# The second layer's modulation moves from the first routing stage into the heads of the first attention

## The reference, cut to what matters

```python
for i in range(2):                                   # layers of the first block
    mod_l = cond_lat @ w_mod[i] + b_mod[i]           # 1 x 6144, split in six
    mod_c = cond_ctx @ w_mod[i] + b_mod[i]
    a_lat = rmsnorm(x, norm_mix_g[i]) * (1 + sc1) + sh1
    y_lat = mla(a_lat, a_ctx) if i == 0 else short_conv(a_lat)   # 8 heads; 256 queries, 512 keys
    x = x + g1 * y_lat
    f_lat = rmsnorm(x, norm_ffn_g[i]) * (1 + sc2) + sh2
    x = x + g2 * hier_moe(f_lat)                     # softmax routing, 32 experts, top 2
...
```

## Time and profile before

| | |
|---|---|
| device time, median of 3 executions | 2698.28 us (2694.34 to 2699.42) |
| the profiled execution | 2698.76 us, span 2697.0 us |
| TensorE products (PE) | 2328.4 us busy, 86% of the span |
| TensorE weight loads (PEld) | 1548.8 us, 57% |
| VectorE (DVE) | 1045.7 us, 39% |
| ScalarE (ACT) | 717.4 us, 27% |
| GpSimd (POOL) | 170.6 us, 6% |
| mean granted TensorE clock | 0.914 of full |
| HBM read | 613.76 MB, 228 GB/s over the span |

### The profile page before, as it was taken

One profiled execution on the slowest core, in us unless ns is written; L12 is line 12 of the kernel. 1 busy time (PEld: TensorE's weight loads), 2 busy tenths in 40 slices (PEclk: granted clock), 3 DMA queues, 4 the chain that ended last, 5 costly groups with the idle time before them and its releaser, 6 DMA issues. The chain is left out here.

```text
span 2697.0 us, 31599 instructions
## 1 busy us (share of the span) xinstructions
PE 2328.4 (86%) x13732; PEld 1548.8 (57%) x13732; DVE 1045.7 (39%) x1713; ACT 717.4 (27%) x1028; POOL 170.6 (6%) x118
## 2 busy tenths in 40 slices
PE   4887799999999784999999979955499989858988
PEld 1633534444444682444444449933389889747988
DVE  3323221111111542111111145733659836654983
ACT  3122211111111431111111135611235424223551
POOL 0000000000000000000000000021005400000540
PEclk7999799999999896999999989965599999988999
DMA  7713599999996433999999925500045443401542
GB/s 260 234 63 125 191 411 421 421 419 398 400 401 246 172 120 152 407 399 398 401 400 398 396 96 187 170 20 0 0 136 183 166 174 132 150 1 63 188 172 79
DMA packets 197633, 616.95 MB, mean 229 GB/s; under 512 B 19952, under 2 KB 82672, under 8 KB 148080
## 3 DMA queue, kind: packets, MB, share of 16 engines
q1 hardware_dynamic: 190416, 610.96, 59.4%
q10 hardware_dynamic: 7072, 3.88, 0.5%
HBM read 613.76 MB, written 1.05 MB: 228 GB/s over the span
## 5 line engine op out<-in xcount | busy, mean ns | idle before, releaser
L517 PE MATMUL bank<-normed_rounded,ring_rounded 128*128 128x256 f32 x3784 | 478.6, 288 | 23.2 <-ACT normed_rounded L581 16.4
L517 PEld LDWEIGHTS bank<-normed_rounded,ring_rounded 128*128 128x128 f32 x3784 | 467.1, 193 | 33.4 <-issue 20.2
L1136 PE MATMUL bank<-ring,arena 128*64 128x512 f32 x2048 | 450.4, 592 | 1.6 <-DVE arena L1500 1.6
L294 DVE TENSOR_TENSOR ring_rounded<-ring,ring_rounded 128x4096 fp32r<-128x4096 f32 (+2 forms) x74 | 326.5, 4416 | 191.5 <-ACT ring_rounded L288 191.5
L517 PE MATMUL bank<-arena_rounded,ring_rounded 128*128 128x256 f32 (+1 forms) x2576 | 359.4, 297 | 33.6 <-ACT arena_rounded L609 12.3
L517 PEld LDWEIGHTS bank<-arena_rounded,ring_rounded 128*128 128x128 f32 x2576 | 334.2, 196 | 50.9 <-ACT arena_rounded L609 14.6
L1136 PEld LDWEIGHTS bank<-ring,arena 128*64 128x64 f32 x2048 | 147.4, 137 | 292.8 <-issue 290.8
L288 ACT ACTIVATE ring_rounded<-ring 128x4096 fp32r<-128x4096 f32 (+2 forms) x74 | 259.7, 3514 | 76.0 <-DMA ring<-in_ffn_w_down 52.9
L1505 DVE TENSOR_TENSOR arena<-arena,bank 64x512 f32<-64x512 f32 x64 | 43.4, 679 | 578.5 <-ACT arena L1337 578.5
L1145 PE MATMUL bank<-ring,arena 128*64 128x512 f32 x1024 | 233.8, 598 | 0.0
L505 PEld LDWEIGHTS bank<-mats,arena 128*128 128x128 f32 (+1 forms) x900 | 117.8, 185 | 101.1 <-issue 79.5
(11 more groups left out here) (222 smaller groups left out, 1870.0 us busy)
## 6 DMA issues: line engine op xcount, KB each, us to landing
ring<-in_moe_w_gate SPq DMA_DIRECT2D x128, 1024.0 KB, 8.6
ring<-in_moe_w_up SPq DMA_DIRECT2D x128, 1024.0 KB, 10.8
ring<-in_moe_w_down SPq DMA_DIRECT2D x128, 1024.0 KB, 7.9
ring<-in_w_mod SPq DMA_DIRECT2D x24, 2048.0 KB, 13.0
ring<-in_ffn_w_up SPq DMA_DIRECT2D x44, 1024.0 KB, 7.4
ring<-in_ssm_w_in SPq DMA_DIRECT2D x12, 2048.0 KB, 8.0
ring<-in_ffn_w_down SPq DMA_DIRECT2D x10, 2048.0 KB, 7.9
ring<-in_conv_w_in SPq DMA_DIRECT2D x6, 2048.0 KB, 9.2
```

The lines of the kernel that those rows point to most:

```text
L294: e.tensor_tensor(ring.rounded[slot][:, 0:n].bitcast(F32R), ring.slots[slot][:, 0:n], ring.rounded[(self.number + 1) % RING][:, 0:n], ALU. ...
L517: end = e.matmul(out, lhs.bitcast(F32R), rhs.bitcast(F32R), start=start and n == 0 and k == 0, stop=stop and n == 2 and k == n_k - 1)
L1136: ends[i] = e.matmul(bank[rows, :], self.xt[x][:, j, n * cap:(n + 1) * cap], weights[:, j, :], start=n == 0 and j == 0, stop=n == 1 and j ...
```

## The change

The twelve steps of layer 1 become a third `Modulation`, `self.ahead` in `Mla`, and the five last steps of layer 0 and these twelve are dealt to the heads in order, two to a head (three in head 7). The first of a head's steps stands where the one step stood, between `scores(h + 1)` and `values(h)`; the second stands inside `values(h)`, between the transposes of the probabilities and the product with V. Head 2 holds the last step of layer 0 with its closing turn, and then step 0 of layer 1. `Moe` of layer 0 has no steps any more. `w_ukv`, whose slot of the ring is read by every head, is *kept*: `fetch` skips that slot until `kept` is cleared behind the `w_o` chunks. The rows of layer 1's steps are held in `late` (two buffers) in place of two in the arena.

```diff
 class Ring:
     def restart(self):
+        self.kept = set()
...
 class Chunk:
     def fetch(self, e, w):
         ring = self.ring
+        while {(ring.number + n) % RING for n in range(2 if self.split else 1)} & ring.kept:
+            ring.number += 1
         self.number = ring.number
...
+    def keep(self):
+        self.ring.kept.add(self.number % RING)
...
 class Modulation:
-    def __init__(self, k, layer, first, steps, row):
+    def __init__(self, k, layer, first, steps, row, *busy):
+        self.busy = busy
...
         if at - 2 >= self.first:
             w.wait_ge(*k.pe.at("mod turn", self.layer, at - 2))
+        elif self.busy:
+            w.wait_ge(*k.pe.at(*self.busy[at - self.first]))
...
 class Mla:
+        self.ahead = Modulation(k, 1, 0, 12, lambda at: late[at % 2], ("mod turn", 0, 10), ("mod turn", 0, 11))
+        between = [(self.rest, at) for at in range(7, 12)] + [(self.ahead, at) for at in range(12)]
+        self.between = [between[2 * h:2 * h + 2 if h < MLA_HEADS - 1 else None] for h in range(MLA_HEADS)]
...
     def sync(self, e, w):
         self.w_ukv.fetch(e, w)
-        for at in range(7, 12):
-            self.rest.fetch(e, w, at)
+        self.w_ukv.keep()
+        for modulation, at in sum(self.between, []):
+            modulation.fetch(e, w, at)
         for chunk in self.w_o:
             chunk.fetch(e, w)
+        k.ring.kept.clear()
...
     def tensor(self, e, w):
+        def steps(h, which):
+            for modulation, at in self.between[h][which]:
+                modulation.step_tensor(e, w, at)
+                if modulation is self.rest and at == 11:
+                    modulation.close_tensor(e, w)
+
         def values(h):
...
                 end.then_inc(*pe.up("pt", h, q))
+            steps(h, slice(1, None))
             bank, emptied = banks.next(dve, "o", h)
...
                 scores(h + 1)
-            if h < 5:
-                self.rest.step_tensor(e, w, 7 + h, turn=True)
+            steps(h, slice(0, 1))
             values(h)
-        self.rest.close_tensor(e, w)
+        self.ahead.close_tensor(e, w)
...
     def scalar(self, e, w):
         for h in range(MLA_HEADS):
-            if h < 5:
-                self.rest.step_scalar(e, w, 7 + h)
+            steps(h, slice(0, 1))
             if h == MLA_HEADS - 1:
                 self.w_o[0].round_scalar(e, w)
             values(h)
+            steps(h, slice(1, None))
             if h + 1 < MLA_HEADS:
                 softmax(h + 1)
-        w.wait_ge(*pe.at("mod turn", 0, 11))
+        w.wait_ge(*pe.at("mod turn", 1, 11))
         self.w_o[1].round_scalar(e, w)
...
 class Moe:
-        self.ahead = None
-        if layer == 0:
-            mod_rows = [ar.take(512), ar.take(512)]
-            self.ahead = Modulation(k, 1, 0, 12, lambda at: mod_rows[at % 2])
...
     def sync(self, e, w):
-        if self.ahead:
-            for at in range(12):
-                self.ahead.fetch(e, w, at)
...
     def tensor(self, e, w):
-        fill(0, 2)
...
-        fill(2, 5)
...
-        fill(7, 5)
-        if self.ahead:
-            self.ahead.close_tensor(e, w)
```

More of the change, by code:

```diff
@@ L715, in sync @@
     def sync(self, e, w):
+        k = self.k
         for at in range(3):
@@ L907, in values, with steps @@
                              ACT.Copy).then_inc(*act.up("pt", h, q))
+        def steps(h, which):
+            for modulation, at in self.between[h][which]:
+                modulation.step_scalar(e, w, at)
         w.wait_ge(*dve.at("turned", (1, 5)))
@@ L1005, in values, with sums @@
             dve.mark("o", h)
+        def sums(modulation, at):
+            modulation.step_vector(e, w, at)
+            if at == 11:
+                modulation.close_vector(e, w)
         self.rest.step_vector(e, w, 5)
@@ L1012, in vector @@
                 key_part(h + 1)
-            if h < 5:
-                self.rest.step_vector(e, w, 6 + h)
+            for modulation, at in self.between[h - 1] if h else [(self.rest, 6)]:
+                sums(modulation, at)
             if h == MLA_HEADS - 1:
@@ L1019, in vector @@
                 softmax(h + 1)
-        self.rest.step_vector(e, w, 11)
-        self.rest.close_vector(e, w)
+        for modulation, at in self.between[-1]:
+            sums(modulation, at)
         self.w_o[1].rest_vector(e, w)
@@ L1167, in tensor @@
         k.meet(w, self.before)
-        def fill(first, n):
-            if self.ahead:
-                for at in range(first, first + n):
-                    self.ahead.step_tensor(e, w, at)
-        fill(0, 2)
         n_log = GROUPS + EXPERTS
@@ L1302, in scalar @@
                     ).then_inc(*self.router.up("router"))
-        def fill(first, n):
-            if self.ahead:
-                for at in range(first, first + n):
-                    self.ahead.step_scalar(e, w, at)
         w.wait_ge(*dve.at("mod", layer, 4 if layer == 0 else 0))
@@ L1324, in scalar @@
             e.activation(x, x, ACT.Exp).then_inc(*act.up(key, "exp", name))
-        fill(2, 10)
         def rows(x):
@@ L1378, in vector @@
             e.tensor_scalar(self.slots[:, n * cap:(n + 1) * cap], count[:, 0:cap], 1.0, None, ALU.add).then_inc(*dve.up())
-        def fill(first, n):
-            if self.ahead:
-                for at in range(first, first + n):
-                    self.ahead.step_vector(e, w, at)
-        fill(0, 1)
         n_log = GROUPS + EXPERTS
@@ L1453, in vector @@
         tt(by_token[:, 1], by_token[:, 1], self.tmp, ALU.add)
-        fill(1, 5)
         bank = banks.of(key, "ranks")
@@ L1485, in vector @@
         places(1)
-        fill(6, 6)
-        if self.ahead:
-            self.ahead.close_vector(e, w)
         def turned_back(x):
```

## The result

| | before | changed |
|---|---|---|
| median, first measurement | 2698.28 us | 2712.29 us (2705.70 to 2715.73, 5 runs) |
| ratio | | 1.0048, 95% interval 1.0030 to 1.0066 |
| second measurement, another chip | 2700.03 us (25 runs) | 2706.49 us (2703.11 to 2715.34, 12 runs) |
| ratio | | 1.0028, 95% interval 1.0012 to 1.0044 |
| profiled execution | 2698.76 us, span 2697.0 | 2708.74 us, span 2706.9 |

The change makes the kernel slower, by 14.0 us in one measurement and 6.5 in the other; 6.8 was forecast. The first value lies 0.3 us outside the forecast's range, the second well inside it. (The ratios are estimated over the runs; they are not exactly the quotients of the two medians.) I read the profiled pair (10.0 us apart) from the stages that were changed to those that were not.

A forecast was written before the change was run, and what follows sets the result against it. It took the attention as bound by a chain through all engines, layer 0's routing first by the router's transfers. Attention +20.7, routing -12.9, convolution start -6.2, layer 1's logits +5.2: +6.8, thus 2705.6 profiled, median 2705.1 us; range 2696 to 2712.

The forecast's parts named there:

- A step ahead costs 2.4: In an attention head, a step placed ahead of the transposes costs 2.4 us, with nothing hiding it.
- A second step costs 1.7: In heads 0, 1, 3 and 4, a step behind the transposes: 2.44 us less 0.74 of TensorE's wait, 1.7 each.
- Head 2: Closing turn waiting for a ScalarE copy, some 0.8 us, then a step without a turn, 1.2: 2.0 in all.
- a head that gets both: Heads 5 and 6, without steps before, get one ahead of and one behind the transposes: 4.1 us each, 8.2 together.
- I had let the clock only gain: Rival: fuller attention heads lose their half-clock stretches, -5.1 us, giving 2700.0; chance 0.22.
- The heads together: All added steps in the attention's heads cost 17.0 us, bounds 15 and 19.
- The end of the attention: w_o's second chunk lands 9.3 us after issue, delaying rounding and TensorE's return by 3.7 us; bounds 2.3 and 7.3.
- The routing of layer 0: Without steps, 35.5 us from logits to first expert; router lands 19.4 after issue, 2.4 later than before: gain 12.9.
- The Trainium skill's rule: Router of layer 0: larger neighbouring rows would delay its landing to 329.7, making the sum 5.2 us higher than forecast.
- The ring's shift: Convolution's first chunk comes earlier, gaining 6.2 us; two more halves ahead of layer 1's router cost 5.2.
- The sum: Whole kernel: 20.7 - 12.9 - 6.2 + 5.2 = +6.8 us on the profiled 2698.76.

The follow-up runs named there:

- b1: Changed kernel with both layers' router weights fetched at the start of the attention, into a free end of the arena: 2657.32 us (0.9843).
- b2: Kernel before the change with both layers' router weights fetched at the start of the attention: 2659.55 us (0.9861).
- c3: Changed kernel with w_o's second chunk in ring slots 0 and 1, so twelve expert halves are issued ahead of the router: 2714.02 us (1.0060).
- a2: Changed kernel with the ring moved one slot on behind the attention, so the convolution's first chunk is in slot 5 again: 2711.96 us (1.0046).
- a3: Kernel before the change with only the ring moved one slot back, so the convolution's first chunk goes to slot 4: 2697.79 us (0.9998).
- a1: Changed kernel measured again, unaltered, on another chip against the kernel before: 2706.49 us (1.0028).
- b4: Changed kernel with both steps of each head ahead of the transposes, none between them and the product with V: 2716.93 us (1.0063).
- a4: Changed kernel with the first steps of heads 0 to 6 moved between the next head's key product and its scores: 2684.22 us (0.9951).
- b3: Changed kernel with first steps between key product and scores, and router weights fetched at the start of the attention: 2639.24 us (0.9783).
- c4: Changed kernel with first steps between key product and scores, router weights fetched early, and w_o's second chunk in slots 0 and 1: 2634.55 us (0.9762).
- c1: Kernel before the change with its five head steps moved between the next head's key product and its scores: 2686.12 us (0.9948).
- c2: Kernel before the change with its head steps between key product and scores, and router weights fetched early: 2644.05 us (0.9802).

## Why the forecast held, point by point

- *A step ahead costs 2.4.* Held: 14.2 - 11.7 = 2.5, and nothing under the key wait.
- *A second step costs 1.7.* Too much: 15.5 - 14.2 = 1.35 at full clock. The 0.74 of ScalarE's wait went as expected, and 0.35 more. The rows place it: from its start to the product with V the second step with its turn takes 188.12 - 185.77 = 2.35 and not 2.44, the wait it fills is 0.81 from start to start, the product with V itself is 0.10 shorter without a wait ahead of it, and the wait ahead of the scores is 2.65 in place of 2.75. Four heads give 5.4 in place of 6.8. Head 2 gave 2.0 as forecast (17.81, less 1.6 for the clock and 14.2), and a head that gets both 15.53 - 11.71 = 3.8 in place of 4.1.
- *The heads together.* From head 1's scores to head 7's it is 14.2 us more (100.26 against 86.09); the forecast's terms for this stretch give 12.9. Steps at full clock account for 5.4 + 2.0 + 3.8 = 11.2, and the half-clock stretches, four of 1.6 in place of two of 1.7, for 3.0. That the stretches grow in number stands in none of my rivals: I had let the clock only gain. So two errors stood against each other here, steps 1.7 too dear and stretches left out; that the total came near is luck.
- *The end of the attention.* The second chunk landed 7.7 us after its issue, not 9.3, and was waited for by 4.78 us. From head 7's scores to TensorE's return it takes 35.9 us in place of 30.0, of which 3.8 are head 6's steps: 2.1 for the end where 3.7 was forecast and 2.3 was the lower bound. With 7.7 in place of 9.3 the forecast's own sum gives the 2.1. The mean at the end of the stage, L550 before and L560 now, is 21.6 us later, 0.9 of which the execution brought along from its start: 20.7, as forecast. It came out of parts that were each a little off: 18.0 for the heads with head 6, not 17.0; 2.1 for the end, not 3.7; and 0.6 from TensorE's return to the mean (23.9 against 23.3), where nothing was forecast. That the whole fits to the tenth is luck.
- *The routing of layer 0.* From the router's issue to the first expert 54.4 us in place of 67.8: 13.4 gained, 12.9 forecast. Landing 19.5 (19.4 forecast), 34.9 from there (35.5). That steps lay under the router's wait is shown by b1 and b2, as 6.4 us.
- *The Trainium skill's rule* (DMA: Bandwidth & Descriptors, Queues, rings and completion order). The page states that an engine changes between queues by whole packets. The prediction concluded from it that the router would land 24.6 us after its issue, as in layer 1, because of the larger rows beside it. It landed after 19.5. The halves are the same ones in both layers and in c3, and the landing of the larger transfer goes from 19.5 to 29.5 us with the number of halves in line, so here the end of the backlog decided. The rule is not refuted: the smaller transfer took no longer behind twelve halves than behind ten, and among the w_mod chunks with their smaller rows both came through sooner. No run here varied the rows' size with the backlog held.
- *The ring's shift.* -6.0 at the convolution's start (the mean comes 896.86 - 883.11 = 13.75 us behind the last row of the experts, L1184 now, in place of 19.7) and +5.0 in layer 1, both as forecast, and both shown by a2 and a3 one at a time.
- *The sum.* 20.7 - 13.4 - 6.0 + 5.0 = +6.3. The profiled pair shows 8.0 at layer 1's first expert less the 0.9 of its start, so 7.1; the convolution took 1.2 more in this execution, from its mean to the router's issue, and from the logits to layer 1's first expert it was 0.4 less. Behind that the pair differs by 2.0 in untouched stages. The first measurement's 14.0 is not explained by the sum: no trace is kept of its other executions, so that the rest lies in the clock and in untouched stages is likely from the spread, and not shown.

## What to carry to other kernels

Work that is dealt out to idle time costs nothing only where the idle time ends last. In these heads TensorE was idle for a quarter of the time; a step behind the scores cost its full length, and the same step a few instructions earlier, ahead of the wait for the key copy, cost nothing. Where work is moved out of a stage, ask what wait had covered it: the twelve steps were worth 19.8 us in the routing and gave 13.4, because a small transfer behind a large backlog was late either way, and that transfer, not the steps, was the 40 us to be had. And a moved slot of a shared ring reaches stages that the change does not name.

## What I had not expected of the hardware

- The half-clock stretches follow the bare waits of about 2.7 us, not the amount of work. Head 1's scores wait 1.6 us, those of heads 2 to 7 wait 2.65 to 2.75. Of these six waits three were followed by a stretch at half clock in the kernel before and five in the changed kernel; the same attentions in other profiled executions have three (a3) and four or five (a1, a2). With the same work and six waits of 2.75 us (b4) it was three. Behind a filled wait there was none, in a4, b3 and c4 as in c1 and c2. What is left there stands behind a wait of 2.65 to 2.75 that had stayed: one stretch each in a4, b3 and c4 with one such wait, one in c1 and two in c2 with two. Each adds 1.6 to 1.7 us. Which of the waits get one differs between executions, and why more do with a second step in the head is not shown.
- In b2 the 32 products of the logits took 3.66 us, at a granted clock of 1.00; in b1 and in the changed kernel 7.0, at 0.50. In b2 two steps stand right ahead of them, and the clock had risen by their end (0.58 over the two together); in the others a wait stands there, of 4.05 and 22.86 us.
